# Second block's latent attention: probabilities scaled before they are turned, two heads weighed in one group, the output kept in turned form

## Reference, cut to what matters

```
def mla_attention(q, k, v):
    ...
    sc = jnp.einsum('bqhd,bkhd->bhqk', q_blk, k).astype(jnp.float32) * scale
    p = jax.nn.softmax(sc, axis=-1).astype(v.dtype)
    return jnp.einsum('bhqk,bkhd->bqhd', p, v)
...
    mixed = jnp.concatenate([
        rms_norm(out_a, out_norm[:A_WIDTH]),
        rms_norm(out_b, out_norm[A_WIDTH:A_WIDTH + B_WIDTH]),
        rms_norm(out_c, out_norm[A_WIDTH + B_WIDTH:]),
    ], axis=-1)
    x = x + jnp.einsum('bsc,cd->bsd', mixed, w_out)
    x = x + expert_choice_moe(rms_norm(x, norm_ffn), w_router, b_router, w_gate, w_up, w_down)
```

## Time and profile before

| | |
|---|---|
| median of 3 runs | 1951.92 us (1950.29 to 1956.62) |
| the profiled execution | 1950.8 us, span 1949.0 us |
| PE, DVE, ACT, POOL busy | 85%, 37%, 15%, 7% of the span |
| chain that ended last | PE 55%, DMA 38%, DVE 4% of the span |
| bytes moved | 599.75 MB, mean 308 GB/s |
| granted TensorE clock | 0.931 over the span |

### The profile page before, as it was taken

How to read it: one execution, slowest core, us unless ns; L and a number is a source line. 1 busy time by engine, 2 the same in 40 slices (tenths; PEclk the granted TensorE clock), 3 DMA queues, 4 the chain that set the end, 5 groups by cost and what they waited for, 6 DMA issues and landing times.

```text
span 1949.0 us, 24582 instructions
## 1 busy us (share of the span) xinstructions
PE 1653.9 (85%) x10472; PEld 944.9 (48%) x10472; DVE 711.9 (37%) x1486; ACT 286.0 (15%) x773; POOL 142.2 (7%) x149
## 2 busy tenths in 40 slices
PE   8999999999899999999785766757999785766757
PEld 3455988544579974574432232322574432232322
DVE  1583566978528986264110010101164110010101
ACT  1142000010611000253000010001253000010000
POOL 0011000000213410220000000000220000000000
PEclk9999999999999999999997888979999997887978
DMA  9991888755225743745999999999845999999998
GB/s 352 344 332 40 275 279 296 283 197 192 95 87 181 252 154 107 223 173 236 391 428 431 426 431 427 433 428 410 266 173 229 377 429 432 423 433 428 432 430 352
DMA packets 164164, 599.75 MB, mean 308 GB/s; under 512 B 18928, under 2 KB 78064, under 8 KB 140272
## 3 DMA queue, kind: packets, MB, share of 16 engines
q1 hardware_dynamic: 163838, 598.03, 77.9%
q10 hardware_dynamic: 242, 0.53, 0.1%
HBM read 594.75 MB, written 3.80 MB: 307 GB/s over the span
## 4 chain that ended last, share of the span: by engine, by line
PE 55%; DMA 38%; DVE 4%; ACT 1%; issue 1%; POOL 0%; SPq 0%; DVEq 0%; ACTq 0%
DMA extra<-in_w_down 14%; DMA extra<-in_w_up 12%; DMA extra<-in_w_gate 11%; PE ps L1255 9%; PE ps L1368 6%; PE ps L1321 6%; PE ps L1293 5%; PE ps L1608 5%; PE ps L948 4%; PE ps L1114 4%; PE ps L1209 3%; PE ps L1506 3%; PE ps L1628 1%; DMA ring<-in_w_mod 1%; PE ps L834 1%; DVE extra L2364 1%
## 5 line engine op out<-in xcount | busy, mean ns | idle before, releaser
L1608 PE MATMUL ps<-ring,wide 128*32 128x256 f32 x2912 | 222.3, 472 | 116.2 <-DMA ring<-in_w_up 69.9
L1608 PEld LDWEIGHTS ps<-ring,wide 128*32 128x32 f32 x2912 | 107.8, 134 | 224.4 <-DMA ring<-in_w_up 79.3
L1628 PE MATMUL ps<-ring,wide 128*32 128x512 f32 x768 | 156.8, 636 | 47.9 <-DMA ring<-in_w_down 47.9
L3194 DVE TENSOR_TENSOR wide<-ps,wide 128x512 f32<-128x512 f32 x16 | 10.7, 670 | 507.0 <-PE ps L1608 507.0
L1255 PE MATMUL ps<-hT,ring 128*128 128x256 f32 (+1 forms) x1088 | 183.8, 330 | 0.0
L1255 PEld LDWEIGHTS ps<-hT,ring 128*128 128x128 f32 x1088 | 166.6, 191 | 17.3 <-issue 2.9
L1608 PE MATMUL ps<-extra,wide 128*32 128x256 f32 x1056 | 88.7, 507 | 63.2 <-DMA extra<-in_w_up 37.5
L1368 PE MATMUL ps<-ring,hT 128*128 128x512 f32 (+2 forms) x320 | 127.3, 555 | 0.4 <-issue 0.4
L1628 PEld LDWEIGHTS ps<-ring,wide 128*32 128x32 f32 x768 | 44.8, 116 | 155.9 <-issue 123.6
L2364 DVE SCALAR_TENSOR_TENSOR extra<-ring,sc,extra 128x512 f32<-128x512 f32 x140 | 109.8, 784 | 5.2
L1608 PEld LDWEIGHTS ps<-extra,wide 128*32 128x32 f32 x1056 | 42.4, 144 | 108.4 <-DMA extra<-in_w_up 41.3
(11 more groups left out here) (370 smaller groups left out, 2099.9 us busy)
## 6 DMA issues: line engine op xcount, KB each, us to landing
ring<-in_w_gate SPq DMA_DIRECT2D x24, 4096.0 KB, 31.3
ring<-in_w_down SPq DMA_DIRECT2D x24, 4096.0 KB, 33.5
ring<-in_w_up SPq DMA_DIRECT2D x20, 4096.0 KB, 33.3
ring<-in_w_mod SPq DMA_DIRECT2D x24, 2048.0 KB, 13.1
ring<-in_w_up SPq DMA_DIRECT2D x44, 1024.0 KB, 7.9
extra<-in_w_gate SPq DMA_DIRECT2D x8, 4096.0 KB, 35.1
extra<-in_w_up SPq DMA_DIRECT2D x8, 4096.0 KB, 33.0
ring<-in_w_in SPq DMA_DIRECT2D x13, 2048.0 KB, 12.6
```

Of the source, the lines that this page charges most:

```text
L1608: last = mm(ps[2 * part + e // 2][j * CAP:(j + 1) * CAP, e % 2 * 2 * P:(e % 2 + 1) * 2 * P], xsT[:, k, e * CAP:(e + 1) * CAP], expert_row( ...
L1628: last = mm(ps[6 + n][e * CAP:(e + 1) * CAP, :], hidT[:, e, k, :], expert_row(n0, e, k)[:, n * N:(n + 1) * N], start=k == 0, stop=k == KD - 1)
```

## The change

For the latent maps (6 to 11) only:

- DVE takes the reciprocal of the row sums right after the exponentials (`inverse`), and GpSimd multiplies the whole 128 x 512 map by it in place (`scale`), before `flip`, which now waits for that.
- `weigh` is replaced by `weigh_two`: the 64 value columns of a head stand as weights, and the turned probabilities (256 columns) stream, for two heads whose results go to partitions 0 to 63 and 64 to 127 of one bank. The output so comes out already turned (channels by tokens). Three such calls replace six; two stand in the loop at m = 8 and 10, the third behind the first `out2`.
- DVE reads each result twice (`far_read`): a plain copy to `far_squares`, and a copy with the output gain to `far_rows`, which `out2` uses directly. The six FAR transposes and ACT's and DVE's copies of them go.
- The sums of squares of the FAR columns: GpSimd squares the three plain copies (and adds the first two), and PE multiplies the squares by a column of ones, four products of width 1. DVE copies the sums (`far_sums`), GpSimd makes 1/sqrt.
- The NEAR transposes stand ahead of flip(11), no longer behind weigh(10). ACT's last `pt_copy` stands behind its copies of the NEAR pieces.
- SP's wait for `pair(2)` and `once_part(0)` is for the third `weigh_two`, and that for `once_part(1)` is for the NEAR transposes.

```
             def flip(s, pre, m, blocks):
-                pe.wait_ge(*s.at("att_probs_ready", m + 1))
+                if m < NAH:
+                    pe.wait_ge(*s.at("att_probs_ready", m + 1))
+                else:
+                    pe.wait_ge(*s.at("b1_scaled_or_summed", m - NAH + 1))
...
+            def weigh_two(s, j):
+
+                m = NAH + 2 * j
+                pe.wait_ge(*s.at("att_probsT_ready", m + 2))
+                pe.wait_ge(*s.at("att_out_read", NAH + j - 1))
+                for kc in range(2):
+                    for e in range(2):
+                        last = mm(ps[2 + j % 2][HD * e:HD * (e + 1), 0:T], vb[:, kc, 2 * j + e, :],
+                                  pT[:, (m + e) % 2, :].rearrange("p (c k t) -> p k c t", c=2, k=2)[:, kc, :, :],
+                                  start=kc == 0, stop=kc == 1)
+                last.then_inc(s.up("att_values_done"), 1)
...
+                    if NAH + 2 <= m < MAPS2 and m % 2 == 0:
+                        weigh_two(s, (m - NAH) // 2 - 1)
...
-                out2(4, NEAR, 0, 0).then_inc(s.up("b2_out_done"), 1)
-                pe.wait_ge(*s.at("att_out_read", MAPS2))
-                for i, (_, _, col) in enumerate(FAR):
-                    for c in range(2):
-                        o = ((i + 1) % 2) * T + c * P
-                        last = nc.tensor.transpose(ps[6 + (i + 1) // 2][:, o:o + P], proj2[:, c, col:col + P], ident)
...
+                out2(4, near, 0, 0).then_inc(s.up("b2_out_done"), 1)
+                weigh_two(s, MLH // 2 - 1)
+                out2(5, near, 0, 1).then_inc(s.up("b2_out_done"), 1)
+                pe.wait_ge(*s.at("att_probsT_ready", MAPS2))
+                pe.wait_ge(*s.at("att_out_read", VALUES2))
+                pe.wait_ge(*s.at("b1_scaled_or_summed", MLH + 1))
+                for c in range(2):
+                    for j in (0, 2):
+                        last = mm(ps[7][:, c:c + 1], far_squares[j][:, c * P:(c + 1) * P], ones[:, 0:1], start=j == 0, stop=j == 2)
+                last.then_inc(s.up("b2_out_flipped"), 1)
...
-                gained(NEAR[4:5], 6, 0, "b2_out_by_act")
-                act.wait_ge(*s.at("att_out_read", MAPS2))
-                mixed_squares((2,), pT[:, 0, :])
-                act.wait_ge(*s.at("b2_out_flipped", 5))
-                gained(FAR[1:3], 7, 0, "b2_out_by_act")
+                gained(NEAR[4:5], 5, 0, "b2_out_by_act")
+                pt_copy(s, "b2_", MAPS2 - 1, 512)
...
-                for i in range(2):
-
-                    pool.wait_ge(*s.at("b2_mixed_sumsq", i + 1))
-                    inv_root(s, 6, "invN", "eps6", "b2_mixed_rstd", ssm, rsm[i], tmpm[i])
+                def scale(m):
+                    pool.wait_ge(*s.at("b1_dots_or_rden", m - NAH + 1))
+                    v = sm[:, m % 3, :].rearrange("p (c k) -> p c k", c=2)
+                    gp.tensor_tensor(v, v, rden[:, 2 * m:2 * m + 2].unsqueeze(2).to_broadcast([P, 2, T]), ALU.mult)\
+                        .then_inc(s.up("b1_scaled_or_summed"), 1)
+
+                for m in range(NAH, NAH + 3):
+                    scale(m)
+                pool.wait_ge(*s.at("b2_mixed_sumsq", 1))
+                inv_root(s, 6, "invN", "eps6", "b2_mixed_rstd", ssm, rsm[0], tmpm[0])
+                for m in range(NAH + 3, MAPS2):
+                    scale(m)
+                for j in range(MLH // 2):
+                    v = far_squares[j]
+                    pool.wait_ge(*s.at("att_out_read", NAH + j + 1))
+                    gp.tensor_tensor(v, v, v, ALU.mult).then_inc(s.up("b1_scaled_or_summed" if j == 2 else None), 1)
...
...
+                def inverse(m):
+                    dve.wait_ge(*s.at("att_probs_ready", m + 1))
+                    nc.vector.reciprocal(rden[:, 2 * m:2 * m + 2], den[:, 2 * m:2 * m + 2])\
+                        .then_inc(s.up("b1_dots_or_rden"), 1)
+
+                def far_read(j):
+                    v = ps[2 + j % 2][:, 0:T]
+                    dve.wait_ge(*s.at("att_values_done", NAH + j + 1))
+                    cp(far_squares[j], v).then_inc(s.up(), 1)
+                    ts(far_rows[j], v, c2(L, "out_norm", FAR[j]), None, ALU.mult).then_inc(s.up("att_out_read"), 1)
```

More of the change, by code:

```diff
@@ L1491, in _ @@
                                 o = (i % 2) * T + c * P
-                                last = nc.tensor.transpose(ps[(0, 1, 6)[i // 2]][:, o:o + P], proj2[:, c, col:col + P], ident)
+                                last = nc.tensor.transpose(ps[(0, 1, 5)[i // 2]][:, o:o + P], proj2[:, c, col:col + P], ident)
                             if i in (1, 3, 4):
                                 last.then_inc(s.up("b2_out_flipped"), 1)
-                    if m >= 1:
-                        h = m - 1
-                        v = (lambda kc: proj2[:, kc, VA2 + HD * h:VA2 + HD * (h + 1)]) if h < NAH else \
-                            (lambda kc: vb[:, kc, h - NAH, :])
-                        weigh(s, "b2_", h, blocks, v)
+                    if m < MAPS2:
+                        flip(s, "b2_", m, blocks)
+                    if 1 <= m <= NAH:
+                        weigh(s, "b2_", m - 1, blocks, lambda kc: proj2[:, kc, VA2 + HD * (m - 1):VA2 + HD * m])
                 def out2(bank, parts, c, n):
                     wt = slot2(B2_AT[("out", n)]).rearrange("p (k n) -> p k n", k=KD)
-                    for i, (k, at_, _) in enumerate(parts):
-                        last = mm(ps[bank][:, :], h8[:, at_, c * P:(c + 1) * P], wt[:, k, :],
+                    for i, (k, lhs) in enumerate(parts):
+                        last = mm(ps[bank][:, :], lhs[:, c * P:(c + 1) * P], wt[:, k, :],
                                   start=i == 0, stop=i == len(parts) - 1)
                     return last
+                near = [(k, h8[:, at_, :]) for k, at_, _ in NEAR]
+                far = [(k, far_rows[j]) for j, k in enumerate(FAR)]
                 for n in range(2):
@@ L1567, in _ @@
                 flip_rows(0)
-                out2(7, FAR, 1, 1).then_inc(tile_done, 1)
+                pe.wait_ge(*s.at("b1_dots_or_rden", MLH + 1))
+                out2(7, far, 1, 1).then_inc(tile_done, 1)
                 pe.wait_ge(sems["router_loaded"], 16)
@@ L3068, in _ @@
                         mask2(m + 1)
+                    if NAH <= m < MAPS2:
+                        inverse(m)
                     if m == MAPS2 - 2:
@@ L3129, in _ @@
                 near_add(0, 0)
-                dve.wait_ge(*s.at("b2_out_flipped", 4))
-                gained(FAR[0:1], 6, T, "b2_out_by_dve")
                 near_add(0, 1)
+                far_sums()
                 near_add(1, 0)
```

67 lines of the change are left out of this document (36 added, 31 removed), and 1 row of the table B1_COUNT.

## The result

| | before | changed |
|---|---|---|
| median of 8 runs each | 1951.64 us (1948.26 to 1956.62) | 1958.99 us (1954.71 to 1970.86) |
| ratio of the changed to before | | 1.0046, interval 1.0027 to 1.0066 |
| the profiled execution | 1950.8 us, span 1949.0 us | 1958.93 us, span 1956.8 us |

The change made the kernel slower by 0.46%. That is more than the 0.3% that can be told from no change, though the interval begins at 0.27%. The time is inside the forecast range, but 2.5 us beyond the forecast, and on the side (slower by over 0.3%) to which I had given 0.35.

What follows compares the result with a forecast made beforehand. It took the chain through PE to bound these stages, not transfers. Loop 1.0 plus output stage 1.3 us a layer, 4.6 for two, gave 1955.4 from the profiled execution, 1956.5 us as median (0.24% slower); range 1949.5 to 1961.5.

Steps and rivals of the forecast that it cites:

- GpSimd's scaling: Latent maps: multiplying 128 x 512 by a broadcast column takes 1.10 us, ends 1.04 and 1.70, entering the chain three times.
- The rival that needs 1.31: Slower by GpSimd: the 128 x 512 scaling takes 1.3 us or more, 1960.1 us in all at 1.70; chance 0.27.
- The two-head product: Latent weighing on PE: two heads run side by side, about 1.03 us in place of 1.68.
- one after the other: Rival, slower by PE: the heads run in sequence, 1.72 + 0.16 us a product, 1959.9 us in all; chance 0.04.
- The waits of the maps: Latent loop: PE waits for ACT's copies at both products and idles 1.6 us for GpSimd before flip(9).
- PE's work decides: Rival, faster: GpSimd and ACT run further ahead, PE's own work gives -1.66 us a layer, 1948.6 us; chance 0.13.
- the 1/sqrt is placed where it costs most: GpSimd's NEAR 1/sqrt, 1.88 us, stands between the scalings of maps 8 and 9, delaying map 9.
- Late by 1.0 us: Latent-map loop: the first output product starts at 883.95 us, before at 882.93.
- The output stage, 1.3 us: Output stage, a layer: adds 1.03 (third product) and 0.95 (sums), loses 0.66 (transposes), uncovered since PE never idles there.
- The transfers: Next transfers released at about 889.3 instead of 882.53 us; the 6.8 us are covered by the queue empty from 900.
- taken up by the transfers: Rival, no effect: the transfer-bound stage takes up the delays, 1951.9 us; chance 0.06.

Runs made afterwards that it cites:

- the swapped loops: Changed kernel with the two-head product's loops swapped, both products of one head first, then the other's: 1962.41 us, median of 2 runs, ratio 1.0055.
- the filled kernel: Changed kernel plus products of the identity that nobody reads, put where PE idles among the latent maps: median 1959.24 us, ratio 1.0029.
- the kernel with three repairs: Changed kernel with the 1/sqrt one map earlier, convolution squares ahead of exps(6) and exps(7), third FAR square added by GpSimd: 1953.93 us, ratio 1.0011.
- DVE's scaling moved: Kernel with three repairs, with DVE's four NEAR scalings moved from beside GpSimd's scaling of map 10 to ahead of map 11's mask: 1954.31 us, ratio 1.0026.
- the kernel with the earlier squares: Changed kernel with ACT's squares of the convolution columns moved from ahead of exps(8) to ahead of exps(6) and exps(7): 1953.40 us, ratio 1.0014.

## Why the prediction was right or wrong

**GpSimd's scaling: right.** 1.04 us, with 1.14 beside DVE's scaling of the NEAR columns; the near row of 0.612 with its step gave 1.04, and I had taken 1.10. The estimate of 1.27 us in the prediction is 0.23 above it, and some 0.16 of it was a dispatch time for which no row stands. The rival that needs 1.31 falls, though the time ended on its side. That the scaling enters the chain three times is not shown: left out altogether it gave back 1.5 us a layer, less than two times 1.04, and waits for ACT stood in its place.

**The two-head product: right.** 1.01 us in the chain, 1.08 with its tail; 1.03 was taken. The rival "one after the other" falls with it, and the swapped loops show that the order of the instructions is not what makes them run side by side.

**The waits of the maps: right up to flip(9).** PE waited for GpSimd there (1.15 us; 1.6 forecast) and for ACT ahead of both products. The rival "PE's work decides" falls with these waits.

**"The squares' sums were ready long before; the 1/sqrt is placed where it costs most": wrong.** One map earlier the loop is as long (32.57 against 32.50 at full clock). I had followed the wait to the instruction ahead of it on GpSimd, and not asked what flip(10) waits for once that is gone: the reciprocal that stands behind score(11), which stands behind flip(8).

**"Late by 1.0 us": this is the step that failed.** Its mechanism is there, smaller than I had it: 0.75 us a layer. It can be checked in the changed kernel's own trace, with every instruction after 878.21 at its full-clock time: flip 0.67, copy 0.61 with 0.04 between and behind, product 1.02, flip 0.49, and then the 2.55 us that I had from the transposes to the output product. That gives 883.6, which is 0.8 late. What the sum lacks is **a term for the granted clock**. I read "both at full granted clock" and priced every instruction of the stage at it, while the same working had PE idle for some 2 us (up to the first two-head product at 874.7) and then 1.6 us where before it idled for 0.68. The three places that the lower clock lengthened are in the chain: the second product, flip(10) and the transposes take 1.62, 1.05 and 1.51 us, where in the filled kernel's chain they take 1.08, 0.59 and 0.89. The difference is 1.6 us, as much as filling the idle time took away (1.64 / 1.54). It fits the fall's length: 3.4 us at half the clock do what 1.7 us do at full clock, so the fall could cost 1.7 at most.

The Trainium skill (TensorE: Matmul & The Clock Gate, What's actually happening) says that the throttled state is the default and that activity releases it. The traces here agree in direction: idle time alone, in the kernel before, put the clock at 0.50.

**The output stage, 1.3 us: right in size, by errors that cancel.** It took 1.44 / 1.45. The sums of squares cost 0.79 in place of 0.95 (eight instructions at 0.10), the third product 1.01 and the transposes gave 0.66 back; the output products sum to 25.44 us in place of 25.13, and that 0.31 had no term. It lies right behind the two interruptions: the 10 instructions behind the third product take 4.49 us and the 38 behind the sums 16.42, where the kernel before takes 0.429 an instruction in its long run (20.60 for 48), so 4.29 and 16.31. Why is open.

**The transfers: right.** SP released the next group at 890.81 us where 889.3 was forecast and 882.53 was before; the queue was still empty between 910 and 915 us, and the group behind it was issued at 915.95, when an output product had freed its slot, as at 912.22 before. The gap ahead of it was shorter than before, as the queue was now busy at 900 to 905 us, but it had not closed:

```profile
890.81 0.37 SPq L756 DMA_DIRECT2D extra<-in_w_gate  x1
```

```profile
900.00:905.00 5.00, 5.00 (x14) 1.00 1.01 424
...
910.00:915.00 5.00, 5.00 (x19) 1.00 0.00 0
```

The rival "taken up by the transfers" falls: the delays of the two stages sum to 7.55 us, the span grew by 7.8 and the median by 7.35.

**The account.** Forecast 2 x (1.0 + 1.3) = 4.6 us. Measured in the stages: 1.5 from the loop's mechanism, 3.2 from the clock, 2.9 from the output stage, together 7.6. Without the clock's 3.2 us the measured 7.35 would be 4.2, or 0.21%, on the side of no change, to which I gave 0.59: the sum came near for the loop's waits and the output stage, and missed by the clock.

**Not in the prediction: DVE beside GpSimd.** I asked whether GpSimd would be slowed by DVE. The cost is mostly the other way round: GpSimd 1.04 to 1.14, one DVE instruction 0.34 to 1.13, because it began second and ended only 0.15 us behind GpSimd. In the changed kernel it is off the path; in the kernel with three repairs it is what the loop waits for. The Trainium skill (GPSIMD Engine Reference, Specifications) says that GpSimd shares its memory interface with VectorE and contends with VectorE's instructions in a 2-port mode or with two SBUF inputs. The trace agrees that there is contention, for a float32 multiplication from SBUF to SBUF; in which mode VectorE ran it, no row shows. The mask of map 11, which reads PSUM, ran beside GpSimd's scaling of map 9 (877.12 us) and kept its 0.69 us, and so did the maxima behind it.

**What stays open.** How much idle time, and how placed, lowers the clock. PE's waits in this stage of 2.00, 1.15 and 0.69 us were followed by a fall in both layers; 2.00 and 0.84 in neither; 0.89, 1.15 and 0.69 in neither. But with the two heads one after the other it fell in layer 2 behind 2.00 alone; with the 1/sqrt moved it fell in layer 1 behind 2.00 and 0.42, and not in layer 2 with 1.99, 0.41, 0.84 and 0.42; and with DVE's scaling moved, both layers had waits of 0.9, 0.42, 0.84 and 0.97, and it fell in the first alone. So the waits make a fall possible and don't decide it, and each kernel's two layers in one profiled execution are a small sample. That the clock's 1.6 us a layer is in the whole time too is seen in the kernel with the earlier squares, whose loop is 2.7 us a layer shorter (1.1 of it the squares') and whose span is 5.5 us shorter; in the filled kernel the executions differ too much among themselves to tell. The 0.6 us of the span outside the three stages are not explained.

## What to carry to other kernels

Where a change makes PE wait in a stage that ran at full clock, price two things: the wait, and the instructions behind it at half the clock. Here the second (1.6 us a layer) was twice the first (0.75), and one wait 1.1 us shorter gave it back in both layers of the profiled execution.

A wait taken away from one engine uncovers the next one. Before crediting it, follow the next flip's data back through every engine, and through what stands ahead of it there.

Before a stage is rebuilt, look for what holds it now. One block of squares on ACT and one uneven split of copies were worth 1.35 us a layer in the kernel before, and the rebuilt stage never reached that.

## What the runs showed of the hardware that was not expected

- Within a dense stage, idle stretches of 2.00, 1.15 and 0.69 us were followed by 3.4 us at a granted clock of 0.50, and so, once, was one of 2.00 alone. One of 3.30 us (and a further delay one map later) was followed by 13.6 us at 0.50 in one layer and 6.8 in the other, through windows of 2 us in which PE was busy for all of them.
- Eight instructions with 64 columns of weights each, four to either column half, take 1.01 to 1.02 us for 256 streamed columns, in either order.
- A one-column product costs 0.10 us an instruction (0.79 for eight), so four of them are no small change in a stage without idle time; halving their number took 0.45 us off.
- A DVE multiplication of 128 x 256 float32 from SBUF to SBUF went from 0.34 to 1.13 us when it began under a GpSimd multiplication of 128 x 512, and ended 0.15 us behind it; GpSimd's own went only from 1.04 to 1.14. DVE instructions that read PSUM (0.69 us) were no longer beside it.
